# A two-block transformer kernel: the causal depthwise convolution moved wholly to TensorE

## The reference, cut to what matters

```python
def conformer_conv(u, conv_w, conv_b, ln_g, ln_b):
    a, g = jnp.split(u, 2, axis=-1)
    h = a * jax.nn.sigmoid(g)
    h = jnp.pad(h, ((0, 0), (CONV_KERNEL - 1, 0), (0, 0)))      # 30 zeros ahead of token 0
    y = lax.conv_general_dilated(h, conv_w[:, None, :], window_strides=(1,), padding='VALID',
                                 dimension_numbers=('NWC', 'WIO', 'NWC'),
                                 feature_group_count=CONV_WIDTH)  # depthwise, 512 channels, 31 taps
    y = y + conv_b
    return jax.nn.silu(layer_norm(y, ln_g, ln_b))
```

## Time and profile before

| | |
|---|---|
| median of 3 runs | 2688.22 us (2686.71 to 2689.08) |
| span of the profiled execution | 2685.7 us |
| TensorE busy | 2603.2 us, 97% |
| VectorE busy | 1169.9 us, 44% |
| ScalarE busy | 437.8 us, 16% |
| GpSimd busy | 108.9 us, 4% |
| mean granted TensorE clock | 0.993 |

### The profile page before, as it was taken

One profiled execution on the slowest core, in us unless ns is written; L12 is line 12 of the kernel. 1 busy time (PEld: TensorE's weight loads), 2 busy tenths in 40 slices (PEclk: granted clock), 3 DMA queues, 4 the chain that ended last, 5 costly groups with the idle time before them and its releaser, 6 DMA issues.

```text
span 2685.7 us, 48043 instructions
## 1 busy us (share of the span) xinstructions
PE 2603.2 (97%) x20457; PEld 1654.4 (62%) x20457; DVE 1169.9 (44%) x2752; ACT 437.8 (16%) x996; POOL 108.9 (4%) x142
## 2 busy tenths in 40 slices
PE   7899999989999999999999998999989999999998
PEld 6659974865333333333333386699459957876993
DVE  5746665663011010010110166466656665354675
ACT  2230000232011011010110213201041001032000
POOL 1000000000000000000000011000000000040001
PEclk9899999999999999999999999999999999999999
DMA  7566555867999999999999936255505554132552
GB/s 227 197 201 207 164 168 196 282 214 274 326 420 418 419 411 418 413 410 419 411 415 417 398 135 105 70 167 165 178 23 175 164 175 134 63 95 64 187 164 88
DMA packets 237949, 642.96 MB, mean 239 GB/s; under 512 B 19769, under 2 KB 153281, under 8 KB 206896
## 3 DMA queue, kind: packets, MB, share of 16 engines
q1 hardware_dynamic: 230320, 618.03, 62.1%
q0 software_dynamic: 6752, 20.51, 3.4%
q10 hardware_dynamic: 672, 1.41, 0.1%
HBM read 626.82 MB, written 13.08 MB: 238 GB/s over the span
## 4 chain that ended last, share of the span: by engine, by line
PE 90%; DVE 6%; DMA 1%; issue 1%; ACT 1%; POOL 0%; DVEq 0%; ACTq 0%; POOLq 0%
PE pacc L1318 14%; PE pacc L1392 11%; PE pt L1017 10%; PE pacc L1409 7%; PE pt L1392 7%; PE pt L1318 6%; PE pacc L1356 6%; PE pada L1418 4%; PE po L1392 3%; PE pt L1356 3%; PE pacc L1257 3%; PE pt L1295 2%; PE pt L1815 2%; PE pacc L1080 2%; PE pacc L1200 2%; PE po L1356 1%
## 5 line engine op out<-in xcount | busy, mean ns | idle before, releaser
L2700 DVE TENSOR_TENSOR gateb<-kT,pt 128x512 f32<-128x512 f32 (+1 forms) x32 | 19.9, 621 | 524.1 <-PE pt L1392 523.4
L1017 PE MATMUL pt<-ring,hT 128*128 128x256 f32 x832 | 186.0, 383 | 3.3 <-DMA ring<-in_w_in 1.7
L1409 PE MATMUL pacc<-ring,bigc 128*32 128x512 f32 x1536 | 182.4, 592 | 0.0
L1017 PEld LDWEIGHTS pt<-ring,hT 128*128 128x128 f32 x832 | 157.8, 191 | 29.4 <-issue 6.2
L1318 PE MATMUL pacc<-probT,prob 128*128 128x128 f32 x1440 | 170.6, 275 | 0.0
L1318 PEld LDWEIGHTS pacc<-probT,prob 128*128 128x128 f32 x1440 | 165.6, 192 | 0.0
L1392 PE MATMUL pacc<-ring,bigc 128*32 128x384 f32 (+1 forms) x1536 | 147.3, 539 | 0.0
L1356 PE MATMUL pacc<-prob,chunks 128*128 128x512 f32 x282 | 136.3, 592 | 0.0
L1392 PE MATMUL pt<-ring,bigc 128*32 128x384 f32 (+1 forms) x1280 | 131.6, 529 | 2.6 <-DMA ring<-in_moe_w_up 2.6
L2486 DVE TENSOR_TENSOR prob<-ring 128x512 f32<-128x512 f32 x86 | 59.5, 692 | 153.4 <-PE pacc L1318 107.1
L1409 PEld LDWEIGHTS pacc<-ring,bigc 128*32 128x32 f32 x1536 | 49.9, 110 | 114.9 <-issue 114.3
(11 more groups left out here) (487 smaller groups left out, 4219.9 us busy)
## 6 DMA issues: line engine op xcount, KB each, us to landing
ring<-in_moe_w_down SPq DMA_DIRECT2D x96, 1024.0 KB, 11.2
ring<-in_w_gate_up SPq DMA_DIRECT2D x66, 1024.0 KB, 5.1
ring<-in_w_ada SPq DMA_DIRECT2D x48, 1024.0 KB, 5.5
ring<-in_moe_w_up SPq DMA_DIRECT2D x48, 768.0 KB, 12.9
ring<-in_w_down SPq DMA_DIRECT2D x33, 1024.0 KB, 4.9
ring<-in_moe_w_gate SPq DMA_DIRECT2D x32, 1024.0 KB, 18.3
ring<-in_moe_w_up SPq DMA_DIRECT2D x32, 1024.0 KB, 19.1
ring<-in_moe_w_gate SPq DMA_DIRECT2D x32, 768.0 KB, 17.7
```

The lines of the kernel that those rows point to most:

```text
L1017: ins = pe.matmul(t[:, q * 256:q * 256 + n], src[:, k, q * P:q * P + P], w[:, k, 0:n], start=(k == 0), stop=(k == KC - 1))
L1409: ins = pe.matmul(down_main[32 * j:32 * j + 32, :], actT[:, 2 * t + k, 32 * g:32 * g + 32], w[:, k, 512 * h:512 * h + 512], start=(t == k ...
```

## The change

All four chunks go to TensorE. The gated input is written to a DRAM tensor `conv_rows` (512 channels by 288 tokens, with zeros at both ends) and loaded back as `conv_shifts`: partition 32s + c of strip a holds channel 32a + c, shifted by s tokens (s from 0 to 3). A stationary block `conv_diagonals[cc][:, a, m, :]` of 128x32 holds four 32x32 diagonals with taps 4m to 4m + 3. So one matmul of 32 output columns applies four taps to 32 channels, four of them (a = 0 to 3) are a **round**, and eight rounds make one chunk: 32 rounds, 128 matmuls a layer, in place of 31 matmuls of 128x128. GpSimd spreads the taps (`spread_taps`, 128x1024 each) and issues the store and the loads (`store_gated`, `load_shifted`; 8 rows of 284 tokens by 32 partitions each, so one half is a 256 KB store and four loads of 291 KB). The taps themselves are loaded by eight small DMAs on GpSimd's queue in runs of 128 B, and `turn_columns` turns them by 16 transposes in place of 4. The rounds of chunks 0 and 1 stand in the front as new items `v0` and `v1`; those of chunks 2 and 3 run ahead of and beside the attention. They accumulate onto a cleared bank: ScalarE takes each chunk and clears the bank behind it (`take_conv`, two instructions). VectorE's taps and ScalarE's diagonals go. Beside the batches, `conv(i)` now stands ahead of the ada tiles.

```diff
-TENSOR_CHANNEL = 3
-TAPS_AHEAD = 4
-TAPS_BESIDE = (2, 3, 6, 6, 6, 0, 4)
+SHIFTS = 4
+ROUNDS = -(-TAPS // SHIFTS)
+ROUNDS_AHEAD = 4
+ROUNDS_BESIDE = (2, 2, 3, 5)
+CONV_TAKEN_IN = 1
+PADDED = S + TAPS + 1
+REACH = S + SHIFTS * (ROUNDS - 1)
...
-FRONT = ("u0 u2 cols u1 u3 kv q0 ada cmp0 cmp1 q1 ht ada s0 w2 g ada gt s1 hq0 ada hq1 hc hks hkw".split(),
-         "... g ada gt s1 hq0 ada hq1 hc hks hkw".split())
+FRONT = ("u0 u2 cols u1 u3 kv q0 ada cmp0 cmp1 q1 ht ada s0 w2 g ada v0 gt s1 hq0 ada hq1 v1 hc hks hkw".split(),
+         "... g ada v0 gt s1 hq0 ada hq1 v1 hc hks hkw".split())
...
+            for dst, src in tap_loads:
+                pool.dma_start(dst, src).then_inc(params_pool, 16)
             pool.sem_inc(y_free, 1)
+            by_channel = conv_rows.rearrange("(c p) t -> p c t", p=P)
+            for lo, hi in ((0, TAPS - 1), (TAPS - 1 + S, PADDED)):
+                pool.dma_start(by_channel[:, :, lo:hi], free(empty_rows[:, 0:1], [[0, CC], [1, hi - lo]]),
+                               allow_slow_non_contiguous=True).then_inc(conv_moved, 16)
+            def spread_taps(l, cc):
+                pool.tensor_tensor(conv_diagonals[cc], free(cst("fold"), [[0, 4], [0, ROUNDS], [1, 32]]),
+                                   free(convv[:, cc, 0, l, 0:1], [[2 * ROUNDS, 4], [1, ROUNDS], [0, 32]]), ALU.mult)\
+                    .then_inc(conv_weights, 1)
+            def store_gated(l, h):
+                pool.wait_ge(conv_gated, 2 * l + h + 1)
+                pool.wait_ge(conv_moved, conv_moves(2 * l + h))
+                pool.dma_start(by_channel[:, 2 * h:2 * h + 2, TAPS - 1:TAPS - 1 + S], conv_in[:, 2 * h:2 * h + 2, :])\
+                    .then_inc(conv_moved, 16)
+            def load_shifted(l, h):
+                pool.wait_ge(conv_moved, conv_moves(2 * l + h) + 16)
+                for s in range(SHIFTS):
+                    src = rows(conv_rows, 2 * P * h * PADDED + s, [[PADDED, 32], [32 * PADDED, 8], [1, REACH]])
+                    pool.dma_start(conv_shifts[h][32 * s:32 * s + 32, :, :, :].rearrange("p c a t -> p (c a) t"), src)\
+                        .then_inc(conv_moved, 16)
+            def conv_operands(l):
+                spread_taps(l, 0)
+                store_gated(l, 0)
+                spread_taps(l, 1)
+                load_shifted(l, 0)
+                spread_taps(l, 2)
+                spread_taps(l, 3)
+                store_gated(l, 1)
+                load_shifted(l, 1)
...
-                for cc in range(CC):
-                    ins = transpose(t[:, cc * P:cc * P + 2 * TAPS], rowsD[:, cc * P:cc * P + P], 2 * TAPS)
+                for g in range(CC * 4):
+                    ins = transpose(t[:, n * g:n * g + n], rowsD[:, P * g:P * g + P], n)
...
-                        ins = pe.matmul(po[:, S:2 * S], diagonals[k], padded[:, TENSOR_CHANNEL, k:k + S],
-                                        start=(k == 0), stop=(k == TAPS - 1), skip_group_check=True)
+                def conv_rounds(count):
+                    for r in range(rounds_at[0], rounds_at[0] + count):
+                        cc, m = divmod(r, ROUNDS)
+                        if m == 0:
+                            pe.wait_ge(conv_weights, CC * l + cc + 1)
+                            pe.wait_ge(conv_moved, conv_moves(2 * l + cc // 2 + 1))
+                            if cc == 0:
+                                pe.wait_ge(conv_gated, 2 * l + 2)
+                            else:
+                                pe.wait_ge(conv_taken, 2 * (CC * l + cc))
+                        for a in range(4):
+                            ins = pe.matmul(po[32 * a:32 * a + 32, S:2 * S], conv_diagonals[cc][:, a, m, :],
+                                            conv_shifts[cc // 2][:, cc % 2, a, SHIFTS * m:SHIFTS * m + S],
+                                            start=False, stop=(m == ROUNDS - 1), skip_group_check=True)
...
+                    if item in ("v0", "v1"):
+                        conv_rounds(ROUNDS)
...
-                multiply_taps(TAPS_AHEAD)
+                conv_rounds(ROUNDS_AHEAD)
                 pe.wait_ge(qT_ready, due("qT_ready"))
...
+            def take_conv(l, cc):
+                o = COL["conv_b"] + CC * l + cc
+                n = CC * l + cc
+                act.wait_ge(conv_multiplied, n + 1)
+                act.activation(y[:, cc, :], po[:, S:2 * S], ACT.Identity, bias=colA[:, o:o + 1]).then_inc(conv_taken, 1)
+                act.wait_ge(conv_taken, 2 * n + 1)
+                act.activation(po[:, S:2 * S], cst("causal")[:, 0:S], ACT.Copy, scale=0.0).then_inc(conv_taken, 1)
...
                 for j in range(4):
                     exp(1, j)
                 lead = batches[0].ahead
+                if conv is not None:
+                    take_conv(conv, 2)
...
+                    if conv is not None and i == CONV_TAKEN_IN:
+                        take_conv(conv, 3)
...
                 for item in FRONT[l][lead:]:
-                    if item == "kv":
-                        make_diagonals(0, 16)
+                    if item in ("v0", "v1"):
+                        take_conv(l, int(item[1]))
...
-                def taps(count):
-                    for cc, k in taps_left[:count]:
...
                     if item == "kv":
                         take_keys_values()
-                        taps(more)
+                        gated_half(2)
                         continue
...
                     elif item == "u3":
                         tell(u_ready)
-                        taps(more // 2)
-                        gated_half(2)
-                        link(ve.memset(po[:, 0:S], 0.0))
-                        ve.sem_inc(conv_padded, 1)
-                        taps(more - more // 2)
+                        link(ve.memset(po[:, :], 0.0))
```

More of the change, by code:

```diff
@@ L248, in scalar_banks @@
         for item in FRONT[l]:
-            scalar() if item[0] in "qs" else vector({"kv": 2, "cols": 3, "ada": 0, "turn": 0}.get(item, 1))
+            scalar() if item[0] in "qs" else vector({"kv": 2, "cols": 3, "ada": 0, "turn": 0, "v0": 0, "v1": 0}.get(item, 1))
         attend(first_batches(), conv=True)
@@ L600, in build @@
                     stream.append(("tile",) + ada_tile(*next(mods)))
-                elif item in ("turn", "w2", "cols", "ht", "gt", "hq0", "hq1", "hc", "hks", "hkw"):
+                elif item in ("turn", "w2", "cols", "ht", "gt", "hq0", "hq1", "hc", "hks", "hkw", "v0", "v1"):
                     continue
@@ L703, in build @@
                       W["moe_router"][0].rearrange("(k p) e -> p k e", p=P)))
+        tap_loads = []
+        for l in range(2):
+            for j in range(SHIFTS):
+                n = -(-(TAPS - j) // SHIFTS)
+                tap_loads.append((rowsD[ROUNDS * l:ROUNDS * l + n, :]
+                                  .rearrange("m (g s c) -> m g s c", s=SHIFTS, c=32)[:, :, j, :],
+                                  rows(W["conv_w"], (l * TAPS + j) * CW, [[SHIFTS * CW, n], [32, CW // 32], [1, 32]])))
         pos_loads = [(posi[:, t:t + 1], rows(W["positions"], t * P, [[1, P], [1, 1]])) for t in range(QT)]
@@ L1170, in attention @@
                 for i in range(last + 1):
-                    if conv is not None and i == len(TAPS_BESIDE) - 2:
-                        pe.wait_ge(conv_taken, pos.get("conv", 0) + 1)
-                        pos["conv"] = pos.get("conv", 0) + 1
+                    if conv is not None and i == CONV_TAKEN_IN + 1:
+                        pos["conv"] = pos.get("conv", 0) + 2 * CC
+                        pe.wait_ge(conv_taken, pos["conv"])
                     if i:
@@ L1828, in conv_sums @@
                     if i == CONV_SUMS[0]:
-                        pe.wait_ge(conv_ready, due("conv_ready"))
+                        pe.wait_ge(conv_taken, 2 * CC * (l + 1) - 1)
                     else:
@@ L2020, in exps @@
                         act.sem_inc(probT_odd, 1)
-                    if conv is not None and i == len(TAPS_BESIDE) - 3:
-                        o = COL["conv_b"] + CC * conv + TENSOR_CHANNEL
-                        act.wait_ge(conv_multiplied, (conv + 1) * TAPS)
-                        act.activation(y[:, TENSOR_CHANNEL, :], po[:, S:2 * S], ACT.Identity, bias=colA[:, o:o + 1])\
-                           .then_inc(conv_taken, 1)
+                    if conv is not None and i == CONV_TAKEN_IN:
+                        take_conv(conv, 3)
                     if mods_beside:
@@ L2106, in _ @@
                     norm_stats(xv, lambda: mod_rows(FRONT[l][:lead].count("ada")))
-                def make_diagonals(first, last):
-                    if l and first == 0:
-                        act.wait_ge(conv_multiplied, TAPS)
-                    for k in range(first, last):
-                        act.activation(diagonals[k], ident, ACT.Copy,
-                                       scale=convv[:, TENSOR_CHANNEL, l * TAPS + k:l * TAPS + k + 1]).then_inc(conv_diagonal, 1)
                 def gate_half(lo):
```

(8 more changed lines are left out.)

118 lines of the change are left out of this document (47 added, 71 removed).

## The result

The changed kernel takes 2707.43 us (median of 4 runs, 2705.92 to 2708.10) beside 2688.65 us for the kernel before on the same chip: ratio 1.0070, 95% interval 1.0058 to 1.0082. It is **18.8 us slower**. The forecast was 2697, 8.8 us above the 2688.22 known then, with a range that ended at 2706. The sign was right, the size was less than half of what came, and the median lies 1.4 us outside the range. The profiled span went from 2685.7 to 2704.1 us, the mean granted clock from 0.993 to 0.987.

What follows compares the result with a forecast made beforehand. TensorE, busy 97% of the span, was taken to bound the kernel. The terms summed to +9.5 us: 2695.2 on the 2685.7 span, 2697.7 on the median, stated as 2697; own range 2690 to 2705, 8-in-10 range 2683 to 2706.

Steps and rivals of the forecast that it cites:

- TensorE's own work: Convolution rounds replacing 31 taps a layer on TensorE, at 0.14 + 0.43 us a round: +0.7 us for two layers.
- Rival 4: Dear strips: each convolution round pays the 0.14 us counted per portion; 64 rounds add 9, giving 2704; chance 0.04.
- Twelve more transposes: Additional small transposes in `cols` at the start, 0.05 us apiece: +0.6 us (0.3 to 1.9).
- Gaps that go: TensorE's waits before q0, compressed keys, `gt`, head transposes and for ScalarE's take vanish in both layers: -7.4 us (-5 to -8).
- s1 at full clock: Layer 0's s1, slow behind the 1.77 us gap, speeds up once it is filled: -1.7 us (0 to -1.7).
- The wait for ScalarE: Ahead of the attention, chunk 2's rounds wait until ScalarE takes chunk 1: 3.4 and 3.2 us, +6.6 (5 to 7.5).
- the clock behind it: Rounds and compressed scores behind that longer gap may run at 1.2 GHz: +3.0 us, both layers (0 to 7.4).
- Lost filler: Attention batches without taps as cover: some five get one wait for VectorE, +3.0 us (0 to 7.6).
- the rival called a wash: The ScalarE wait comes, but batches and clock stay as they are: +1.8, 2690; chance 0.20.
- The start: Small tap and zero runs meet the load of constants that `cols` waits for: +1.0 us (0 to 6).
- Rival 3: Small runs hold up the constants, moving every piece behind `cols` by 6 us instead of 1: 2703; chance 0.10.
- The DMAs in layer 1: Second half's store and loads delay q1's tile: +2.0 us (0 to 2.8); q1 then runs slow: +1.7 (0 to 3.5).

Runs made afterwards that it cites:

- e6: Changed kernel with the second half's store and loads behind q1's tile, and in layer 1 the first half's loads late as well; ratio 1.0059 to the kernel before.
- e5: Changed kernel with layer 0's small parameter columns turned behind u1 instead of ahead of it; ratio 1.0042 to the kernel before.
- c2: Changed kernel with three moves together, those of e1, e5 and e6; ratio 1.0004 to the kernel before.
- e8: Same kernel as e7, run once more for its timeline; ratio 1.0036, layer 1 467.7 us beside 457.4 before.
- e9: Kernel before, with two ada tiles of layer 1's front moved from beside cmp0 and cmp1 to behind gt and hq0; ratio 0.9992.
- e1: Changed kernel with ScalarE taking chunk 1 and clearing the bank ahead of item s1's root, not behind it; ratio 1.0040 to the kernel before.
- e4: Changed kernel with the padding zeros late as in e3, and the taps loaded in four long-run transfers and sorted in SBUF; ratio 1.0059 to the kernel before.
- e3: Changed kernel with the two transfers of zeros into the padding issued behind the parameter columns, not at the start; ratio 1.0074 to the kernel before.
- e7: Kernel before, with only the change's stores and strided loads added, into a buffer nobody reads; timed at ratio 1.0036, 9.7 us slower.
- e2: Changed kernel with the second half's store and loads held until TensorE is done with q1's tile, both layers; ratio 1.0048 to the kernel before.
- c4: Changed kernel with the moves of e1, e2 and e5, and two of layer 1's ada tiles moved behind gt and hq0; ratio 0.9979 to the kernel before.
- c5: c4 with chunk 2's rounds placed otherwise: one ahead of the attention, others into the gaps around the window keys; ratio 0.9972 to the kernel before.

## Why the prediction was too low, point by point

**TensorE's own work (+0.7): right.** A chunk of eight rounds takes 3.66 us, four rounds 1.93 at full clock; between starts that is the 0.14 + 0.43 a round of the forecast. Rival 4, dear strips, is false. The Trainium skill ("TensorE: Matmul & The Clock Gate", Part 3) gives 2.38 times for three column tiles, and an estimate from that figure is 4.6 us for eight rounds. The measurement decides: four strips of 32 columns with their own weights and rows ran at full gain here.

**Twelve more transposes (+0.6): a little low.** 1.15 to 1.27 us in e6, e5 and c2 against 0.46, so +0.75; 1.89 in the changed kernel, where the granted clock was down.

**Gaps that go (-7.4): right.** Each named bracket is gone, but for 0.15 us of the wait for ScalarE in layer 0.

**s1 at full clock (-1.7): the number came, by luck.** s1 takes 7.15 us. But the gap ahead of it does not by itself slow it: e8 and e9 still have the gap of 1.77, and s1 takes 7.15 there as well. From e8:

```profile
90.15 0.63 PE L1804 MATMUL pt<-const,prob 128*128 128x32 f32 x4 [1.77 <-DVEq L2243]
90.62 7.15 PE L1048 MATMUL pt<-ring,hT 128*128 128x256 f32 x32
```

**The wait for ScalarE (+6.6) and the clock behind it (+3.0): right.** 3.29 + 3.01 = 6.3. From the first of the rounds ahead to the first turn of the attention it now takes 14.54 and 13.80 us, before 13.10 and 13.08 with 0.5 us more work in each layer: +3.1. e1 gives back 8.1 us (runs) or 8.4 (traces, behind `v1`) for the two together.

**Lost filler (+3.0): about right.** Behind the first turn, the portions held 22 taps (10.2 us at 0.465) and now hold 8 rounds (3.7), 6.6 us less work a layer. That stretch to `w_out` became 6.65 us shorter in layer 0 and 5.41 in layer 1, as if only 1.1 us of cover had been lost. But the two waits of 0.56 for ScalarE lay in it, which are booked under the gaps. TensorE's busy time in the stretch, layer 0 and layer 1, before:

```profile
114.30:168.12 53.82, 50.71 (x475) 35.64 (x474) 38.54 (x143) 19.91 (x68) 0.00 (x0) 0.95 0.62 207
568.53:625.52 56.99, 52.60 (x508) 36.93 (x506) 34.94 (x133) 20.64 (x69) 0.00 (x0) 0.95 0.68 234
```

and after:

```profile
126.04:173.21 47.17, 42.59 (x499) 28.33 (x495) 30.79 (x117) 20.95 (x71) 0.00 (x0) 1.00 0.66 229
590.95:642.53 51.58, 47.10 (x530) 30.82 (x527) 31.13 (x117) 21.61 (x72) 0.00 (x0) 0.94 0.75 258
```

Its idle time is 3.1 and 4.4 us before, 4.6 and 4.5 after: +1.6, and without the two waits of 0.56 it is +2.7. What is left, -0.5, is clock: layer 0 no longer has the part at 0.50 there (the granted clock of the stretch went from 0.95 to 1.00). So the rival called a wash was wrong in this point too.

**The start (+1.0): the step "at the start ... meet the load of constants" was mis-sized.** By the start of kv layer 0 was 4.6 us late, of which the transposes are 1.4. The wait itself grew by 1.8 (1.2 because the columns could be turned later, 0.65 because TensorE came earlier), and u1 and u3 behind it took 2.1 us more at reduced clock, which had no term in the sum. That last part is not in every execution (e6, the same up to there, has 14.08 us for u1 and u3; e1 to e4 have 15.9 to 16.9). Rival 3 had named the place and put 6 us on it.

**The DMAs in layer 1 (+2.0, and +1.7 for q1's clock): this is the step that failed**, with the sentence "Chunks 0 and 1 are loaded while tiles have slack in both layers". They have none in layer 1. q1 started 6.0 us later against its layer's start than before, not 2.0, and ran 2.5 us slower, and an ada tile 0.6. The price per megabyte was right for this execution: 6.0 us for 2.85 MB (GpSimd's two stores and eight loads) is 2.1 us per MB, and the forecast worked with 2. Counted from kv, q1 was late by 5.3 us in e1, 6.3 in e5, 8.6 in e3, 8.7 in e4 and 7.6 in e8, so the price runs from 1.9 to 3.1. The bytes were wrong: the sum counted the second half alone, 1.4 MB. The reason given for that, that the first half lands before any tile is waited for, misses that the ring is six tiles deep: SyncE issues a tile when the one six places before is used, and bytes moved twenty microseconds before the wait still push every later tile back. e6 shows it from one side (both halves away, q1 waits 0.38) and e7 from the other (the moves alone, 9.7 us). The time of the second half was off as well. The forecast had its store and loads between 512 and 526; GpSimd stood 9.00 us until the first half's loads had landed, stored at 520.57, and issued the loads when q1's tile was on its way:

```profile
526.48 2.34 POOL L889 DMA_DIRECT2D big<-conv_rows  x4 [5.17 <-DMA conv_rows<-big]
```

**The tile of s0 in layer 0 (nothing forecast): +2.1.** 2.28 against 0.20. With the second half's loads behind q1 (e2) it waits 0.20 again, so they are a condition. They are not the only one: e5 holds nothing back and waits 0.20 too, and with the order of before the same moves cost 0.68 (e8). That the forecast's own gains, the gaps before q0 and the compressed keys, bring TensorE to s0 too soon fits this, but no run shows it by itself.

The terms as measured: 0.7 + 1.4 (transposes, with their slow clock) - 7.4 - 1.7 + 6.3 + 3.1 (clock) + 2.7 (lost cover) - 0.5 (clock in the batches) + 5.0 (waits for tiles ahead of q1) + 3.1 (q1 and an ada tile slow) + 2.1 (tile of s0) + 1.8 + 2.1 (start) - 0.65 (TensorE's earlier arrival) = +18.0, where the two layers together lost 17.0. All of them come from one profile before and one after, so that they close to 1 us says less than the experiments do.

So the convolution's work on TensorE was not itself the loss. Its placement and its transfers were: with one `take_conv` moved, one store with its loads held back, the columns behind u1 and two filler tiles out of the full stretch, the kernel is faster than before (c4, 0.9979). How much of c5's gain is the change, and how much the order alone would give, is not wholly separated: e9 puts the ada tiles' part at about 2 us on the kernel before; moving the columns there was not tried.

## What to carry to other kernels

Where weights stream through a ring of tiles, look for the next place at which TensorE waits for a tile, and charge it with every byte that others move since the ring was last full, not with those in flight at the wait. Delaying the transfer can only move the wait to the next tile; it has to go behind the last tile that TensorE waits for, or a filler tile has to come out of the stretch. And when an engine's queue is written out by hand, a new item belongs ahead of the item that waits for somebody else, not behind it in the order of the list: here that one line was worth 8 us.

## What the runs showed of the hardware that was not expected

**The DMA engines move less in the same busy time while GpSimd's loads run.** In layer 1, between 505 and 515 us the changed kernel moved 193 GB/s at a DMA share of 0.85; before, the share of 0.87 between 510 and 520 went with 269 GB/s. With the second half's loads under way, between 535 and 540, it was 215 at a share of 1.04. The shifted loads (32 partitions by 8 rows of 1136 bytes) landed after 7.3 us in the first half and 11.1 in the second (medians of four), where the store of 256 KB took 5.6.

```profile
kT<-conv_rows POOLq DMA_DIRECT2D x4, 284.0 KB, 7.3
big<-conv_rows POOLq DMA_DIRECT2D x4, 284.0 KB, 11.1
conv_rows<-big POOLq DMA_DIRECT2D x1, 256.0 KB, 5.6
```

**A gap does not always bring the clock down behind it.** e6 and e2 are the same program up to there. e6 waited 2.04 us for the constants and ran u1 and u3 in 14.08 us, e2 waited 2.19 and took 16.15. In e9 a wait of 0.98 was followed by 15.74. Behind the gap of 1.77 in layer 0, s1 took 8.84 us in the kernel before and 7.15 in e8 and e9. And the first projection of layer 0 took 3.81 us in most executions but 5.94, 5.76 and 5.41 in e5, c4 and e8.

**TensorE stops once in the second block for nothing that the profile names**, and the length is not the same from kernel to kernel: 2.25 us before, 2.12 after, 2.03 in e1, 3.48 in e5, 4.93 in e3, 5.50 in c2, where the following piece took 3.78 us for what takes 1.99 elsewhere in that block.

```profile
1662.02 0.48 PE L1056 MATMUL pt<-const,prob 128*128 128x128 f32 x1 [5.50 <-issue]
1662.43 3.78 PE L1148 MATMUL pacc<-kT,qT 64*128 64x512 f32 x8
```

What it waits for stays open. GpSimd's 64 KB transfers of the bias run beside it, and the queue of instructions moves 5 packets in the 70 us or so around it, in the kernel before, in e1 and in c2 alike. The second block differs by up to 8 us between kernels that are the same there (1095.1 to 1103.2 in the table), and in c2 the longer stop and the slower piece behind it are 5 of them. So e6 and c2 look better in their layers than in their time.
